# Sample attention: the first group's value products with compressed and recent values issued ahead of the selected weights

## The reference

```
def nsa_sample(xn, kv_cmp_pages, kv_sel_pages, kv_win_buf, page_table, ...):
    ...
    kc, vc = compress(cmp_all[:, :, 0], ...), compress(cmp_all[:, :, 1], ...)
    ...
    o = nsa_attend(q, q_rot, gates, pos, kc, vc, sel_blk[..., 0, :], sel_blk[..., 1, :], win_all k, win_all v, kw_pos)

def nsa_attend(...):
    p_c = masked_softmax(q @ kc)            # 63 compressed positions
    o_c = p_c @ vc
    imp = p_c @ overlap                     # picks the 16 blocks of 64 that are kept
    p_s = masked_softmax(q_rot @ k_sel)     # 1024 past positions, less one dropped block, and the new one
    o_s = p_s @ v_sel
    p_w = masked_softmax(q_rot @ kw)        # 512 recent positions and the new one
    o_w = p_w @ vw
    o = g_c * o_c + g_s * o_s + g_w * o_w
```

## Time and profile before

| | us |
|---|---|
| median of 3 runs | 1502.36 |
| lowest and highest | 1501.08, 1505.44 |
| the profiled execution | 1502.96 |
| its span, first to last instruction | 1501.3 |
| PE busy | 1462.6 (97%) |
| DVE, ACT, POOL busy | 865.3, 420.0, 364.1 |

### The profile page before, as it was taken

The page is one execution under the profiler, slowest core; times in us unless marked ns, Lnnn a source line. Parts: engine busy times, 40 slices in busy tenths (PEclk is TensorE's granted clock), DMA queues, the critical chain, the costliest instruction groups (busy, mean ns, idle before and its releaser), DMA issues. The chain is left out here.

```text
span 1501.3 us, 25957 instructions
## 1 busy us (share of the span) xinstructions
PE 1462.6 (97%) x9827; PEld 1221.8 (81%) x9827; DVE 865.3 (58%) x1907; ACT 420.0 (28%) x1063; POOL 364.1 (24%) x479
## 2 busy tenths in 40 slices
PE   8999999899999999999999999999999999999998
PEld 7877899555557888888888889788888888888888
DVE  2754443888545795654667735661585556776513
ACT  3011343788520443334200001442531111000012
POOL 0000300467640359991230034280000000000000
PEclk9999999999989999999999999999999999999999
DMA  8346571311595444463344320712312222322201
GB/s 275 110 128 142 170 214 50 102 49 51 162 352 132 156 166 162 143 228 130 116 133 132 121 68 34 304 34 89 109 60 82 87 99 71 113 84 84 85 28 58
DMA packets 142894, 184.36 MB, mean 123 GB/s; under 512 B 31298, under 2 KB 101642, under 8 KB 141746
## 3 DMA queue, kind: packets, MB, share of 16 engines
q1 hardware_dynamic: 139634, 174.31, 35.6%
q0 software_dynamic: 3136, 8.39, 1.7%
HBM read 163.42 MB, written 29.69 MB: 129 GB/s over the span
## 5 line engine op out<-in xcount | busy, mean ns | idle before, releaser
L2679 POOL TENSOR_SCALAR att_p<-att_p,att_tot,gates 128x128 f32<-128x128 f32 (+3 forms) x128 | 79.6, 636 | 44.9 <-DVE att_tot L2601 44.3
L305 PE MATMUL psum<-xT,l_w 128*128 128x260 f32 x384 | 85.3, 383 | 2.0 <-PEq L113 1.8
L1010 PE MATMUL psum<-xT,l_w 128*128 128x260 f32 x384 | 85.2, 383 | 1.6 <-PEq L113 1.6
L305 PEld LDWEIGHTS psum<-xT,l_w 128*128 128x128 f32 x384 | 72.8, 190 | 13.5 <-issue 2.4
L1010 PEld LDWEIGHTS psum<-xT,l_w 128*128 128x128 f32 x384 | 72.8, 190 | 12.9 <-issue 1.8
L1026 PE MATMUL psum<-l_up_t,l_w_sums 128*128 128x260 f32 x336 | 78.2, 382 | 0.0
L2205 PE MATMUL psum<-cmp_xt,cmp_w 64*128 64x256 f32 (+1 forms) x640 | 72.2, 362 | 0.3 <-DVE cmp_xt L2126 0.3
L1026 PEld LDWEIGHTS psum<-l_up_t,l_w_sums 128*128 128x128 f32 x336 | 63.8, 190 | 9.8
L2652 ACT ACTIVATE att_p<-att_p,att_low 128x128 f32<-128x128 f32 (+3 forms) x128 | 70.4, 554 | 2.8 <-DVE att_low L2592 2.8
L1289 ACT ACTIVATE l_hidden<-l_tmp 128x260 f32<-128x260 f32 x64 | 26.6, 420 | 144.9 <-DVE l_tmp L1439 144.8
L2592 DVE CUSTOM_DVE_ANT_0 att_p<-psum,causal 128x128 f32<-128x128 f32 (+3 forms) x128 | 55.7, 487 | 18.7 <-PE psum L2427 18.1
(11 more groups left out here) (607 smaller groups left out, 3175.2 us busy)
## 6 DMA issues: line engine op xcount, KB each, us to landing
l_w<-in_mlp_w SPq DMA_DIRECT2D x16, 2048.0 KB, 7.8
l_w<-in_mlp_w SPq DMA_DIRECT2D x32, 1024.0 KB, 5.3
proj_w<-in_nsa_w_in SPq DMA_DIRECT2D x4, 2048.0 KB, 9.9
cmp_raw<-in_cache_kv_cmp SPq DMA_DIRECT2D x24, 256.0 KB, 3.1
xT<-in_cache_kv_cmp SPq DMA_DIRECT2D x24, 256.0 KB, 2.9
sa_more<-in_cache_kv_sel POOLq DMA_DIRECT2D x44, 128.0 KB, 6.2
sa_more<-in_cache_kv_sel SPq DMA_DIRECT2D x34, 128.0 KB, 7.0
hT<-in_cache_kv_cmp SPq DMA_DIRECT2D x16, 256.0 KB, 2.9
```

Of the source, the lines that this page charges most:

```text
L305: mm = nc.tensor.matmul(ps[:, n % 8, 0:HALF], w[s][:, k, m * P:(m + 1) * P], src[:, kk, cols(h)], start=(kk == 0), stop=(kk == last))
L1010: mm = nc.tensor.matmul(ps[:, n % 8, 0:HALF], w[s][:, k, m * P:(m + 1) * P], src[:, kk, cols(h)], start=(kk == 0), stop=(kk == last))
L2679: ve.tensor_scalar(pr[:, n % PR, par, at:at + w], pr[:, n % PR, par, at:at + w], tot[:, n % PR, u, par:par + 1], c.gates[:, i, gate:gate + ...
```

## The change

Group 0's steps 0 to 5 move ahead of the wait for the selected weights. Step 0 now stands where the twelve matmuls of `keep_awake` stood, the window's `turn_p` follows it at once, then six `keep_awake` matmuls, then steps 1 to 5 as soon as the window's weights have been copied (`p_kept[1]`). So that these steps need not wait for the selected values, the window transfers of sequences 0 to 3 increment two semaphores of their own, `win_landed[0]` (issued by SP, sequences 0 and 1) and `win_landed[1]` (POOL, 2 and 3). `v_landed` of these sequences then counts 8 landings. Step 6 now has its wait for `p_kept[2]` at its head, with the wait for the selected values. Group 1 is as before. DVE, ACT, SP and POOL execute what they did, in the order that they had.

```diff
+        self.win_landed = [c.sem(f"sa_v_win_landed_{e}") for e in ("sp", "pool")]
...
-                eng.dma_start(dst, self.win[b, :, :, KVW:]).then_inc(self.v_landed[b], 16)
+                eng.dma_start(dst, self.win[b, :, :, KVW:]).then_inc(self.win_landed[b // 2] if b < 4 else self.v_landed[b], 16)
...
                 pe.wait_ge(p_kept[0], 1)
-                keep_awake(c, 5, 12)
-                pe.wait_ge(weighed[1], 1)
-                turn_p(1, s_win, s_win[:, WIN:], 6, 0)
-                pe.wait_ge(weighed[2], 1)
-                for h in range(2):
-                    turn_p(2, s_sel, s_sel[:, PAST:] if h == 1 else None, 3 + h, 4 * h)
-
-                for bg in range(2):
-                    for q in range(4):
-                        pe.wait_ge(v_landed[bg * 4 + q], 16 * (NPAGE + 1))
-                    if bg == 0:
-                        pe.wait_ge(p_kept[1], 2)
-                    for i in range(NC_S + 3):
-                        if i == 6 and bg == 0:
-                            pe.wait_ge(p_kept[2], 3)
+                def values(bg, parts):
+                    for i in parts:
                         for q in range(4):
...
+                values(0, range(1))
+                pe.wait_ge(weighed[1], 1)
+                turn_p(1, s_win, s_win[:, WIN:], 6, 0)
+                keep_awake(c, 5, 6)
+                for e in range(2):
+                    pe.wait_ge(cache.win_landed[e], 32)
+                pe.wait_ge(p_kept[1], 2)
+                values(0, range(1, 6))
+                pe.wait_ge(weighed[2], 1)
+                for h in range(2):
+                    turn_p(2, s_sel, s_sel[:, PAST:] if h == 1 else None, 3 + h, 4 * h)
+
+                for bg in range(2):
+                    for q in range(4):
+                        pe.wait_ge(v_landed[bg * 4 + q], 16 * (NPAGE + bg))
+                    if bg == 0:
+                        pe.wait_ge(p_kept[2], 3)
+                    values(bg, range(6 if bg == 0 else 0, NC_S + 3))
```

## The result

The changed kernel takes 1503.16 us in the median of 20 runs (1499.46 to 1505.36), the kernel before 1500.65 (20 runs, 1499.01 to 1505.44). The ratio is 1.0014, with a 95% interval from 1.0008 to 1.002: about 2 us slower (2.5 by the medians), and within the 0.3% that were called no change. The forecast was 1503.1 in a range from 1499.3 to 1506.3. The profiled execution took 1505.12 us, its span was 1503.5.

What follows compares the result with a forecast made beforehand. PE was taken as the bound, with group 1's last transfer landing a close second; -2.9 (earlier start) + 3.4 (low clock) + 0.1 (semaphore waits) = +0.6 us, given as 1503.1 us by the median, range 1499.3 to 1506.3.

Steps and rivals of the forecast that it cites:

- The order on PE and DVE: Group 0: DVE's 1.45 us stall goes, PE itself is late next, and waits about 1.0 us ahead of step 6.
- The landing as the floor: Ahead of group 1: it can't start before its last transfer lands at 449.5, so PE idles 3.8 us.
- rival D: Group 1: the landing isn't the bound, transfers mostly land earlier, the whole 6.75 us is gained, 1495.6; chance 0.03.
- The clock's price: Group 1: the clock falls around 449 to 450 after the wait, costing 3.4 us, between 1.7 and 5.1.
- The term of -2.9 us: Start of group 1: 449.5 instead of 452.43, so only 2.9 of 6.75 us are gained.
- the sum: Whole change: -2.9 + 3.4 + 0.1 = +0.6 us on the profiled execution's 1502.96 us.
- The split of the gain between order and clock: Step 6 starts 4.0 us earlier: 1.85 us from the order, 2.15 from the clock staying at full.

Runs made afterwards that it cites:

- e2: The kernel before with 7 idle matmuls behind the window's transposes and none between the groups: 1501.16 us, ratio 1.0007 to before.
- second profile of before: The kernel before, no edit, profiled again: 29.37 us from the last product with keys to the next part's first matmul.
- e1: The changed kernel with 14 more idle matmuls between group 0 and group 1: 1499.67 us, ratio 0.9999 to before.
- e4: The changed kernel with group 1's products reading group 0's value slots, its landing wait moved behind them: 1496.18 us, ratio 0.9973 to before.
- e5: The changed kernel with the two new semaphores on group 1's window transfers, so its steps 0 to 5 wait only for these: 1496.81 us, ratio 0.9976.
- e7: The changed kernel's order with the old semaphores, early steps waiting for all of group 0's landings: 1502.99 us, ratio 1.0014 to before.

## Why the prediction was right, and where it was not

**The order on PE and DVE: right.** Counted from the last product with keys, the transposes of the selected weights were forecast at 6.4 us (measured 6.41), step 6 at 8.6 (8.72), the wait ahead of it at 1.0 us (1.11). DVE's stall of 1.45 us is gone, and nothing is gained by it: the selected weights are ready at 440.06, and PE is busy until 440.99.

**The landing as the floor: right.** Group 1 starts at 16.3 us (forecast 16.5), after 3.39 us of waiting (3.8). Wherever group 1 waits for all of its values, it doesn't start before 15.4 us (e2), so rival D, the whole 6.75 us by earlier transfers, was not seen. The floor is that of one queue: in the changed kernel's profile POOL's last page is there 2.1 us before SP's. The prediction took the floor as given; moving a page from SP's queue to POOL's was not tried. The clock was low behind the wait in the changed kernel's profiles (0.50 from 450.3 to 457.0 in the first). The rule of the Trainium skill ("TensorE: Matmul & The Clock Gate", section "HAM oscillation — how this bites in real kernels") that a burst behind a DMA wait starts cold agrees with that; behind the shorter wait of 0.93 us in the second profile of before the burst did not.

**The clock's price: right in kind, a little too large.** The term was 3.4 us, between 1.7 and 5.1. The low stretch was 6.7 us long, twice the term, as forecast; e1 measures 2.85. The difference is that its first 0.6 us ran out while PE was still waiting (450.3 to 450.89), where half clock costs nothing.

**The term of -2.9 us: right for the profiled execution, wrong for the median.** In the pair of first profiles the sum closes: group 1 starts 3.15 us earlier (16.31 against 19.46 after the last product with keys) and takes 2.85 longer, which is the 0.3 us between the T's. The step that failed is the last of the sum: "That execution was 0.6 above the median of 1502.36, so against the median I say 1503.1." (A slip as well: 1502.96 less 0.6 is the median, so +0.6 gives 1503.0.) It took the first profile's low stretch of 10.2 us as what the kernel before does. The two further profiles have 3.3 us and none, T's of 29.99 and 29.37, and 20 runs have a median of 1500.65 instead of 1502.36. Against the profiled execution the group's earlier start is real (T 0.3 us less, where the sum said 0.6 more). Against the two others there is nothing to gain: group 1 starts at 15.6 and 16.2 us, within 0.2 us of the landing, and the changed kernel's 16.3 and 16.6 are no earlier. What is left is the clock's price, and the result is +2.5 us in the median where +0.7 was forecast; the range held it because it had been drawn for the other cases too. That 1503.1 hit 1503.16 was luck: the two errors (a base 1.7 us too high, a change 1.8 us too small) cancelled. The mechanism, a wait for the landing and a low clock behind it, was no luck, and e1 and e4 show it.

**The split of the gain between order and clock** (1.85 and 2.15 us up to step 6) didn't matter, as said, while the landing bounds both. Step 6 stands at 10.46 us in the second profile of before, where the clock was full: the order's own share is 10.46 - 8.72 = 1.74.

## What to carry to other kernels

Before work is moved ahead of a wait, look up what the work behind it waits for, and how much earlier that may start: here 1 to 3 us, while 4 to 7 were being made. Time won ahead of a DMA floor turns into one long idle stretch of TensorE, and if the clock falls in it the change costs more than it brings. The same order of group 0 with the semaphores on the group that is late (e5) was 3.8 us faster than before; with them on the group that was early it was no faster than without them (e7). A low clock seen in one profile is not a property of the kernel: profile two or three executions before its removal is counted as a gain.

## What the runs showed of the hardware

A kernel's low clock stretches differ between executions in code that is unchanged: near 280 us the clock was at 0.50 for all of a window of 10 us in the changed kernel and at full in the first profile of before, with PE busy 7.12 and 5.42 us of it (54 and 74 matmul records, which take longer at the lower clock). Behind the same wait of 1.89 us it was low for 10.1 us, for 3.3 us and not at all in three profiles of one kernel. Half clock isn't always lost time: 3.3 us of it in group 0 cost at most 0.6 us, since a wait for data stood behind it (T 29.99 against 29.37), while 6.7 us of it behind the wait cost 2.85 us. Fourteen idle matmuls of 128x128 in the wait (3.39 us) kept the clock at 1.00 in e1.
